# Gate weights of the recurrence in 1 MB loads, fp32 gate steps by row block, and fill steps beside other small products

## What is computed

```python
h = rms_norm(x)
q, k, v, z, gates = split(h @ w_in)          # 2048 x 9120: attention, RWKV-7, two gates
A = sliding_window_attention(q, k, v)        # 16 heads
y = rwkv7(z)                                 # 16 heads of 64: S_t = S (diag(w) - kk (a*kk)^T) + v k^T
merged = sigmoid(gates[0]) * (A @ w_branch_a) + sigmoid(gates[1]) * (y @ w_branch_b)
x = x + merged @ w_out
x = x + experts(rms_norm(x))                 # 32 experts, 2 for each token
out = rms_norm(x)
```

## Time and profile before

| | us |
|---|---|
| median of three executions | 1717.53 |
| their range | 1717.0 to 1720.67 |
| the profiled execution | 1715.85 |
| its span, first to last instruction | 1714.0 |
| TensorE busy | 1428.9 (83%) |
| VectorE busy | 738.0 (43%) |
| ScalarE busy | 433.9 (25%) |
| mean granted clock of TensorE | 0.914 of full |
| bytes read from HBM | 521.8 MB, 308 GB/s over the span |

### The profile page before, as it was taken

One profiled execution on the slowest core, in us unless ns is written; L12 is line 12 of the kernel. 1 busy time (PEld: TensorE's weight loads), 2 busy tenths in 40 slices (PEclk: granted clock), 3 DMA queues, 4 the chain that ended last, 5 costly groups with the idle time before them and its releaser, 6 DMA issues.

```text
span 1714.0 us, 26493 instructions
## 1 busy us (share of the span) xinstructions
PE 1428.9 (83%) x11604; PEld 875.8 (51%) x11604; DVE 738.0 (43%) x1101; ACT 433.9 (25%) x601; POOL 39.3 (2%) x34
## 2 busy tenths in 40 slices
PE   7999999999898899999877687686776866867766
PEld 6888888757767688886232132232322322312322
DVE  6665554578566666543323231322222322322232
ACT  5544444344353344444100000000000000000002
POOL 1000000001103010000000000000000000000000
PEclk9999999999989999999888887888888888888888
DMA  9654456231111493868999999999999999999996
GB/s 349 241 175 168 154 197 221 74 111 51 65 53 62 176 346 136 304 236 341 405 430 433 431 431 431 433 432 431 434 432 429 433 433 431 432 433 432 428 430 289
DMA packets 80411, 529.31 MB, mean 309 GB/s; under 512 B 7712, under 2 KB 10026, under 8 KB 65738
## 3 DMA queue, kind: packets, MB, share of 16 engines
q1 hardware_dynamic: 75488, 514.50, 73.6%
q0 software_dynamic: 2192, 9.35, 1.5%
q10 hardware_dynamic: 2650, 4.26, 0.7%
HBM read 521.80 MB, written 6.29 MB: 308 GB/s over the span
## 4 chain that ended last, share of the span: by engine, by line
PE 53%; DMA 40%; DVE 4%; ACT 2%; issue 1%; DVEq 0%; SPq 0%; ACTq 0%
DMA ring<-in_expert_w_up 14%; DMA ring<-in_expert_w_gate 12%; PE ps L1055 10%; DMA ring<-in_expert_w_down 8%; PE ps L642 8%; PE ps L1164 7%; PE ps L703 5%; PE ps L643 4%; DMA arena<-in_expert_w_up 4%; PE ps L1300 4%; PE ps L743 3%; DMA arena<-in_expert_w_gate 2%; DMA ring<-in_w_in 2%; PE ps L605 1%; PE ps L963 1%
## 5 line engine op out<-in xcount | busy, mean ns | idle before, releaser
L2265 DVE TENSOR_TENSOR arena<-arena,ps 128x512 f32<-128x512 f32 x248 | 153.8, 681 | 408.0 <-PE ps L1152 407.0
L1164 PE MATMUL ps<-ring,arena 128*32 128x512 f32 x1024 | 153.0, 747 | 92.1 <-DMA ring<-in_expert_w_gate 57.6
L1164 PE MATMUL ps<-arena 128*32 128x512 f32 x1018 | 148.3, 729 | 76.2 <-DMA arena<-in_expert_w_up 49.7
L642 PE MATMUL ps<-h_both,w_hi 128*128 128x512 f32 x544 | 193.9, 401 | 1.3 <-DVE w_lo L1829 1.3
L643 PE MATMUL ps<-h_both,w_lo 128*128 128x256 f32 x544 | 153.6, 282 | 0.0
L1164 PEld LDWEIGHTS ps<-ring,arena 128*32 128x32 f32 x1024 | 36.7, 132 | 204.6 <-issue 93.9
L1164 PEld LDWEIGHTS ps<-arena 128*32 128x32 f32 x1018 | 37.3, 129 | 175.8 <-issue 117.3
L642 PEld LDWEIGHTS ps<-h_both,w_hi 128*128 128x128 f32 x544 | 103.0, 189 | 27.1 <-DVE w_lo L1829 1.5
L1887 DVE TENSOR_TENSOR w_lo<-ring,w_hi 128x1024 fp32r<-128x1024 f32 (+1 forms) x62 | 74.3, 1199 | 82.8 <-ACT w_hi L1468 82.5
L1959 DVE TENSOR_TENSOR v_lo<-ring,v_hi 128x1024 fp32r<-128x1024 f32 x64 | 78.3, 1224 | 71.1 <-ACT v_hi L1498 70.9
L1300 PE MATMUL ps<-ring,arena 128*32 128x512 f32 x512 | 85.5, 830 | 27.6 <-DMA ring<-in_expert_w_down 21.2
(11 more groups left out here) (333 smaller groups left out, 2128.9 us busy)
## 6 DMA issues: line engine op xcount, KB each, us to landing
ring<-in_w_in SPq DMA_DIRECT2D x34, 2048.0 KB, 7.8
arena<-in_expert_w_gate SPq DMA_DIRECT2D x15, 4096.0 KB, 32.8
ring<-in_expert_w_gate SPq DMA_DIRECT2D x15, 4096.0 KB, 32.7
arena<-in_expert_w_up SPq DMA_DIRECT2D x15, 4096.0 KB, 32.4
arena<-in_expert_w_down SPq DMA_DIRECT2D x15, 4096.0 KB, 33.4
ring<-in_expert_w_up SPq DMA_DIRECT2D x14, 4096.0 KB, 33.4
ring<-in_expert_w_down SPq DMA_DIRECT2D x14, 4096.0 KB, 35.1
ring<-in_w_out SPq DMA_DIRECT2D x8, 2048.0 KB, 8.1
```

The lines of the kernel that those rows point to most:

```text
L642: mm(out, hi[:, 128 * n:128 * n + 128], both(k), start=start and n == 0, stop=False)
L1164: last = mm(ps[32 * c:32 * c + 32, bank, :], XS[:, k, 32 * j:32 * j + 32], w[c], start=i == 0, stop=i == 3, tile_position=(0, 32 * c))
L2265: last = v.tensor_tensor(xs, xs, ps[:, banks[nb], :], ALU.add)
```

## The change

- The weights of blocks 5 to 7 come in twelve loads of 1 MB, four row blocks each. The first four (two chunks) are issued as before. Each later one is issued once the four row blocks that lay in its place have been used. The second halves of the slots signal on semaphores of their own (`f_sem`).
- The fp32 steps go by row block: both tiles for row block 0, then both for row block 1. The first ring slot is released at step 16, not 24. ScalarE's two evacuations of these tiles move behind its first hi part.
- Fill steps are placed anew: none at 'mt', two each behind 'g' and 'f' in each half (places 'rb' and 'f' of the table); the first half's levels have 3, 2, 2, 2, 2 (before: 3, 2, 2, 3, 0), its 'end' 6 (7); the second half's levels have 2, 2, 2, 1, 1 (3, 2, 2, 2, 2), its 'xl' 1 (2).
- The pieces are made at fewer places: none ahead of 'mt' and none between the levels. The first half's gate tiles 10 and 11 are evacuated behind level 5 instead of within level 4.
- The four 'wl' products come ahead of the four 'a' products.

```diff
@@ -367,3 +367,12 @@
 
-            return 16 * sum(slot_of(i) == slot_of(n) for i in range(n + 1))
+            s = slot_of(n)
+            return 16 * (sum(slot_of(i) == s for i in range(n + 1)) + (3 if n >= NM and s > 1 else 0))
+
+        def f_sem(g):
+
+            return S(f"slot_full{g // 2 % 2 + 2 * (g % 2)}")
+
+        def f_landed(g):
+
+            return landed_by(NG + 2 * GD + g // 2 % 2 - 2 * (g % 2)) + 16 * (g // 4 + 1)
 
@@ -373,6 +382,6 @@
         FILL_A = 2
-        FILL_H = (dict(wl=1, ks=5, vtr=1, bon=6, l=3, mt=2, lv=(3, 2, 2, 3, 0), xl=1, ua=3, s1=1, s2=1, yy=7, end=7),
-                  dict(wl=1, ks=5, vtr=1, bon=6, l=3, mt=2, lv=(3, 2, 2, 2, 2), xl=2, ua=3, s1=1, s2=1, yy=8, end=0))
-        MADE_H = (dict(wl=10, vtr=17, mt=11, bt=17, lv=(0, 19, 0, 19, 24), rb=24, s=25, yy=26),
-                  dict(wl=34, vtr=41, mt=35, bt=41, lv=(0, 43, 42, 43, 47), rb=47, s=48, yy=48))
+        FILL_H = (dict(wl=1, ks=5, vtr=1, bon=6, l=3, mt=0, lv=(3, 2, 2, 2, 2), xl=1, ua=3, rb=2, f=2, s1=1, s2=1, yy=7, end=6),
+                  dict(wl=1, ks=5, vtr=1, bon=6, l=3, mt=0, lv=(2, 2, 2, 1, 1), xl=1, ua=3, rb=2, f=2, s1=1, s2=1, yy=8, end=0))
+        MADE_H = (dict(wl=10, bt=18, rb=24, s=26, yy=27),
+                  dict(wl=35, bt=43, rb=47, s=48, yy=48))
         assert 2 * FILL_A + sum(v if at != "lv" else sum(v) for row in FILL_H for at, v in row.items()) == 2 * UF
@@ -451,7 +460,8 @@
                 load(NG + c, slot(NG + c), cols(GA0 + 512 * (c // 2), c % 2, 512))
-            for c in range(2 * GD + 2, 16):
-                n = NG + c
-                sp.wait_ge(*((S("chunk_used"), n - 1) if n < NF + 2 else (S("w_used"), 4 + F0 + 8 * (n - 1 - NF))))
-                sp.dma_start(ring[:, slot_of(n), :].rearrange("p (k n) -> p k n", k=8), cols(GA0 + 512 * (c // 2), c % 2, 512))\
-                    .then_inc(S(f"slot_full{slot_of(n)}"), 16)
+            for g in range(UF // 4):
+                c = 2 * GD + 2 + g // 2
+                s, o = slot_of(NG + c), 4 * (g % 2)
+                sp.wait_ge(*((S("chunk_used"), NF - 1 + g // 2) if g < 4 else (S("w_used"), 4 + F0 + 4 * (g - 3))))
+                sp.dma_start(ring[:, s, 512 * o:512 * o + 2048].rearrange("p (k n) -> p k n", k=4),
+                             cols(GA0 + 512 * (c // 2), c % 2, 512)[:, o:o + 4, :]).then_inc(f_sem(g), 16)
             wa = a["w_branch_a"][0].rearrange("(k p) n -> p k n", p=P)
@@ -706,3 +716,3 @@
 
-            gate_part = [2 * GD * KT]
+            gate_part = [0]
 
@@ -712,11 +722,10 @@
                 for m in range(gate_part[0], gate_part[0] + count):
-                    tile, k = divmod(m, KT)
-                    b, t = divmod(tile, TT)
-                    n = NG + 2 * b + k // 8
+                    k, t = divmod(m, TT)
+                    n = NG + 2 * GD + k // 8
                     if k == 0:
 
-                        pe.wait_ge(S("gate_out"), tile - 1)
-                    if k % 8 == 0:
+                        pe.wait_ge(S("gate_out"), 2 * GD - 1 + t)
+                    if t == 0 and k % 8 == 0:
                         full(n)
-                    last = mm(ps[:, 6 + tile % 2, :], hT[:, k, 128 * t:128 * t + 128], slot(n)[:, k % 8, :],
+                    last = mm(ps[:, 6 + t, :], hT[:, k, 128 * t:128 * t + 128], slot(n)[:, k % 8, :],
                               start=k == 0, stop=k == KT - 1)
@@ -838,12 +847,10 @@
 
+                for t in range(TT):
+                    mm(ps[:, t, :], lz[0:64, 0, 128 * t:128 * t + 128], wua[0:64, hc:hc + 512], start=True, stop=False)
+                    last = mm(ps[:, t, :], C("ones")[0:1, :], w0row[0:1, hc:hc + 512], start=False, stop=True)
+                last.then_inc(S("half_ps"), 1)
                 for j in range(HJ):
-                    t = j // 2
-                    if j % 2 == 0:
-                        wl = mm(ps[:, t, :], lz[0:64, 0, 128 * t:128 * t + 128], wua[0:64, hc:hc + 512], start=True, stop=False)
-                    else:
-                        wl = mm(ps[:, t, :], C("ones")[0:1, :], w0row[0:1, hc:hc + 512], start=False, stop=True)
-                    al = mm(ps[:, 2 + j // 2, 256 * (j % 2):256 * (j % 2) + 256],
-                            wua[64:128, hc + 128 * j:hc + 128 * j + 128], lz[64:128, 0, :], start=True, stop=True)
-                wl.then_inc(S("half_ps"), 1)
-                al.then_inc(S("half_ps"), 1)
+                    last = mm(ps[:, 2 + j // 2, 256 * (j % 2):256 * (j % 2) + 256],
+                              wua[64:128, hc + 128 * j:hc + 128 * j + 128], lz[64:128, 0, :], start=True, stop=True)
+                last.then_inc(S("half_ps"), 1)
                 fill_mm(fills["wl"])
@@ -991,2 +998,3 @@
                 last.then_inc(S("half_ps"), 1)
+                fill_mm(fills["rb"])
                 for cp, hp, ci, j in pairs:
@@ -996,2 +1004,3 @@
                 last.then_inc(S("half_ps"), 1)
+                fill_mm(fills["f"])
                 pe.wait_ge(S("rb_done"), hh + 1)
@@ -1048,3 +1057,3 @@
 
-            assert gate_part[0] == 2 * (GD + 1) * KT and fill_part[0] == 2 * UF
+            assert gate_part[0] == TT * KT and fill_part[0] == 2 * UF
             def late_unit(left, buf, bank, ks, start, stop):
@@ -1526,3 +1535,2 @@
             exponentials(3)
-            gate_out()
             f_at = [0]
@@ -1533,4 +1541,4 @@
                 for y in range(f_at[0], max(upto, f_at[0])):
-                    if y % 8 == 0:
-                        act.wait_ge(S(f"slot_full{slot_of(NF + y // 8)}"), landed_by(NF + y // 8))
+                    if y % 4 == 0:
+                        act.wait_ge(f_sem(y // 4), f_landed(y // 4))
                     if y >= 8:
@@ -1543,2 +1551,3 @@
             gate_out()
+            gate_out()
             turned_out(2)
@@ -1584,3 +1593,3 @@
                     gate_out()
-                f_hi(made["vtr"])
+                f_hi(made["bt"])
                 act.wait_ge(S("half_ps"), half_at("at", hh))
@@ -1604,7 +1613,6 @@
                         f(U(14)[:, 512 * hp:512 * hp + 512], ps[:, hp, :], ACT.Copy).then_inc(S("v1_done"), 1)
-                    if lv == 4 and hh == 0:
-                        gate_out()
-                        gate_out()
-                    if lv != 3:
-                        f_hi(made["lv"][lv - 1])
+                if hh == 0:
+                    gate_out()
+                    gate_out()
+                f_hi(made["rb"])
                 act.wait_ge(S("half_ps"), half_at("ua", hh))
@@ -2028,3 +2036,2 @@
                 step(v.tensor_tensor(g16(U(14)), g16(U(8)), tile16(C("lvlT", 64)), ALU.mult))
-                f_lo(made["mt"])
                 dve.wait_ge(S("half_ps"), half_at("mt", hh))
@@ -2052,4 +2059,3 @@
                                 .then_inc(S(("x_done", "xt_done")[w]), 1)
-                    if lv > 2:
-                        f_lo(made["lv"][lv - 1])
+                f_lo(made["rb"])
                 dve.wait_ge(S("half_ps"), half_at("rb", hh))
```

## The result

The changed kernel is slower: a median of 1726.46 us (seven executions, 1722.15 to 1736.81) beside 1717.53 (seven, 1714.15 to 1720.67), ratio 1.0059 with an interval of 1.0037 to 1.0081. The forecast of 1710.9 and its range of 1706 to 1717 miss it; nearest stood the slower rival (1722.7), with a chance of 0.06 and at another place. The profiled execution took 1728.98 us, 13.1 more than that of before.

A forecast was written before the change was run, and what follows sets the result against it. Nothing can hide behind 594 us (PE busy, then DMA engines full), so recurrence changes (367 to 594 us) reach the end one for one. Terms sum to -6.6 us: median 1717.53 to 1710.9, range 1706 to 1717.

The forecast's parts named there:

- slower rival: Both halves, 'mt' place that lost its steps: clock falls, 5.9 us a half, total 1722.7 us; chance 0.06.
- Second stall: Second half, wait for gate weights near 480 us: smaller loads remove 2.7 idle and 5.9 half-clock us, -8.6 us.
- rival with a chance of 0.06: Second half stays at half clock although no load is late: 5.9 us kept, total 1716.8 us; chance 0.06.
- Decay first: Both halves, 'wl' ahead of 'a' products: lost overlap costs +0.85 us a half, +1.7; bounds 0 and +1.1.
- The loads: SP's queue: twelve load issues instead of six cost nothing, since each load lands in time.
- Two steps behind each small product: Both halves: eight fill steps, 5.8 us, lie in PE's existing instruction pauses, 0 us; bounds +5.8 and -1.
- rival (+5.8): Small products, both halves: the pauses don't absorb the added steps, +5.8 us, total 1716.7 us; chance 0.12.
- Second half's levels: Second half, level 1 to 'xl': five fill steps fewer save 2.2 us; bounds 0 and -3.6.
- First half to L986: First half, levels to the first small product: lost fill time gains, ScalarE's later copy costs, total +0.4 us.
- First stall: Start of the recurrence: load lands by 367 us, but ScalarE's own order delays its copy to 371.5, +0.8 us.
- Gate tiles: Second half: three fill steps instead of one stand behind the gate evacuations, +1.6 us; bounds +0.4 and +1.9.
- mask products: First half: mask products start 1.5 us earlier without VectorE's piece, but level 1's update gains only 0.3 to 0.5, -0.4 us.

The follow-up runs named there:

- e9: Kernel before with 1 MB loads, no piece or fill step ahead of the mask products, seventh load issued with the eighth: 1707.16 us, ratio 0.9945.
- after: The changed kernel with all parts of the change, against the kernel before: 1726.46 us, ratio 1.0059.
- e11: e9 with the 'wl' decay products ahead of the four 'a' products in both halves: 1713.80 us, ratio 0.9989 of the kernel before.
- e4: Changed kernel with the seventh 1 MB load issued with the eighth, behind the levels: 1721.89 us, ratio 1.0035 of the kernel before.
- e5: Changed kernel with the first branch-weight load held until the second half's small products are done: 1722.10 us, ratio 1.0020 of the kernel before.
- e10: e9 with two fill steps behind each small product of both halves, taken from first-half 'end' and second-half levels: 1714.11 us, ratio 1.0000 of the kernel before.
- e1: Changed kernel with the four 'a' products put back between the 'wl' products: 1719.91 us, ratio 1.0029 of the kernel before.
- e7: e1 with the seventh load and the first branch-weight load both issued later: 1716.87 us, ratio 0.9992 of the kernel before.
- e12: e9 with two fill steps behind each small product of the first half only, taken from its 'end' steps: 1711.33 us, ratio 0.9965 of the kernel before.
- e3: Kernel before with only the twelve 1 MB loads: 1711.59 us, ratio 0.9962.
- e6: e1 with fp32 steps tile by tile and the gate tile ahead of `f_hi`, as before: 1716.50 us, ratio 0.9993 of the kernel before.
- e8: e3 with no piece or fill steps ahead of the mask products, the steps moved to the levels: 1710.99 us, ratio 0.9969 of the kernel before.

## Why the prediction was wrong

Three steps failed: that the second half would run at full clock once the load was in time, the price of decay first, and the loads at nothing.

**Second stall, -8.6: right in size, but not kept.** The load is no longer late, and where the clock holds (e9) the 30.33 us are 22.04, 8.3 less. In after they are 27.75, for the clock fell again with no load late; the rival with a chance of 0.06 said that it would. The forecast took "no idle time ahead" as enough for full clock, by one half of one execution. In the fifteen stretches with the old order and no late load it fell in ten, at a place where half-array products follow one another.

**Decay first, +0.85 a half: mis-sized, since it left out the clock.** The working counted TensorE's time in line; the 'a' products did take turns, as it said. But the eight records took 3.10 and 3.64 us at a falling clock where it put 1.75, and the fall went on into the cumulative sums. By stretches it costs 3.7 us a half and by e11's ratio 7.6 in all, against bounds of 0 and +1.1 a half. The slower rival had this mechanism, at 5.9 a half, but put it at the mt place, which ran at 1.00; nothing was asked about the place where eight products that had run side by side were put in line. That its 1722.7 came nearest is luck.

**The loads, "I take nothing for them": wrong.** It was looked at whether each load lands in time, not what it meets in flight. With the seventh in flight PE pauses for instructions, and it costs 4.0 us in the levels (after against e4); the branch load, issued later against PE's work because the second half's steps had moved, costs 3.9 in the small products (after against e5). In the kernel before that load flew ahead of the small products, at 555.81 to 563, and cost no such pause.

**Two steps behind each small product, 0: right by itself.** Four steps take 0.5 us in the first half of e10, and 12.70 us in e5 is less than the 13.18 before. The rival (+5.8) had the result of after's second half, 3.4, but not the cause. Where half clock fell into the stretch it took 14.14 (e1, e4, e7). What was not looked at is what the steps leave behind: with four 'end' steps fewer the clock fell at the second decay products in both runs (e10, e12), which may or may not be their doing. The change itself takes only one.

**Second half's levels, -2.2: nothing to -1.** After has 25.67 for 25.25, and 0.2 less behind them; e10, with four steps fewer than e9, gives 0.95. From level 1 to level 5 of after PE waits 1.5 us for instructions (1.8 before), 1.1 for VectorE's update and 0.8 for ScalarE's copies (neither before): with the steps gone it waits for the other engines instead.

**First half to L986, +0.4: +4.6**, counted from 'l' (54.3 for 49.7 us), of which 4.0 are the seventh load's. Where both loads are late (e7) it is 50.3, +0.6, so without the load the term was near. Behind level 5 it is +1.7: L993 waited 1.99 for ScalarE's copy, which began at 461.10.

**First stall, +0.8: right** (+0.9; copy at 371.89 for 371.5). But keeping the order would have won 1.5 (e3, e6), so this part of the change costs 2.4.

**Gate tiles, +1.6 and mask products, -0.4: right.** At full clock (e7) the second half takes 17.65 us from the cumulative sums to 'l', where 17.5 was forecast; the first half took 15.91 before. The mask products come 1.5 and 1.7 us earlier; level 2 of the first half gains 0.35 over 'l', since eight pieces (7.10 us) stand ahead of level 1's update. In the second half the mask products' gain stays.

Against the forecast the miss is some 16 us: decay first 5.9 more than booked (e11) and the two loads 6.3 to 7.9 (e7 against e1 by the ratios, e4 and e5 by the stretches) account for 12 to 14 of them. Counted up from e9, decay first (+7.6), the moved steps with the branch load (+7 to +9) and the early seventh load (+4) make 19 to 21; the changed kernel is some 20 above e9. Each of these is uncertain by 3 to 5 us, the fp32 part's 2.4 lies in the same bound, and the half clock at the second decay products is in the first and in the second alike, so that the sum closes is partly chance.

## What to carry to other kernels

A load that nobody waits for can still have a price while it is in flight beside long runs of small products: place its release, not only its landing. Before products are put in line that ran side by side on different rows of the array, look at the clock behind them: TensorE time that nothing waits for can still cost there. Test the parts of a change one by one on the fastest base, since here several losses hid a gain of 9 to 11 us.

## What was not expected of the hardware

- A load of 1 MB or 2 MB in flight can go with a gap of 7.3 to 8.2 us between two 16 KB packets of the instruction queue q8 (among the small products mostly 3.5 to 5, up to 6.9 with no load in flight) and a pause of 1.82 to 2.98 us in runs of 64x64 products (1.70 at most without a load). Where the release of one load was all that differed the stretch cost 4.0 (after, e4), 3.9 (after, e5) and 1.9 us (e8, e9), clock and all. It need not: e3's seventh load went with a gap of 6.2 us and a pause of 0.92.
- The clock can fall to half with PE busy 100% of the time by the trace: 27.57 us busy of 27.57, granted clock 0.81 (e11). By the trace's busy time alone the fall is not to be foreseen.
- The same program has the clock at the same place sometimes at full and sometimes at half (21.62 us in e9 and 26.26 in e12 for one and the same code up to there). One profile doesn't price such a place.
